# Turning the differential probabilities by VectorE squares and a DRAM round trip in a two-layer attention trunk

## The reference

```python
def diff_attention(q, k, v, lam):            # 4 heads, two 64-dim maps per head
    sc = einsum('bqhcd,bkhcd->bhcqk', qb, kf) * scale      # causal, blocks of 128 queries
    p = softmax(where(causal, sc, -inf))
    attn = p[:, :, 0] - lam * p[:, :, 1]
    return einsum('bhqk,bkhe->bqhe', attn, vf)

def dsa_attention(q, k, v, qi, ki, wi):      # 4 heads of 128; an 8-head indexer picks 64 keys a query
    score = einsum('bqhk,bqh->bqk', relu(einsum('bqhd,bkd->bqhk', qib, kif)), wib)
    _, idx = top_k(where(causal, score, -inf), 64)
    p = softmax(q . k[idx] * scale);  return p @ v[idx]

def hybrid_layer(x, ...):
    h = rms_norm(x);  proj = h @ w_in        # 4680 columns: dq dk dv dg sq sk sv sg iq ik iw
    oa = rms_norm(diff_attention(rope(dq), rope(dk), dv, lam)) * (1 - lambda_init) * silu(dg)
    ob = dsa_attention(rope(sq), rope(sk), sv, rope(iq), rope(layer_norm(ik)), iw) * silu(sg)
    return x + rms_norm(concat(oa, ob) @ w_out)
```

## Time and profile before

| | us |
|---|---|
| median of 3 runs | 302.72 (302.6 to 302.75) |
| the profiled execution | 302.85 |
| its span, first to last instruction | 301.1 |
| PE busy | 292.4 (97%) |
| DVE busy | 234.9 (78%) |
| ACT busy | 163.9 (54%) |
| POOL busy | 67.6 (22%) |
| mean granted TensorE clock | 0.996 of full |

### The profile page before, as it was taken

How to read it: one execution, slowest core, us unless ns; L and a number is a source line. 1 busy time by engine, 2 the same in 40 slices (tenths; PEclk the granted TensorE clock), 3 DMA queues, 4 the chain that set the end, 5 groups by cost and what they waited for, 6 DMA issues and landing times.

```text
span 301.1 us, 4401 instructions
## 1 busy us (share of the span) xinstructions
PE 292.4 (97%) x1568; PEld 246.4 (82%) x1568; DVE 234.9 (78%) x474; ACT 163.9 (54%) x284; POOL 67.6 (22%) x116
## 2 busy tenths in 40 slices
PE   8999999999999999999999999999999999999992
PEld 7799777788787888788888988778878788887892
DVE  4752989899999997955984786878999999787343
ACT  5986963736577473603665855473737747390101
POOL 6558210303030220101060740012303030210101
PEclk9999999999999999999999999999999999999998
DMA  7999959457518569860059799937653675742011
GB/s 242 370 371 386 371 214 354 135 143 227 195 69 210 209 211 303 191 201 23 0 158 369 242 350 250 325 108 204 209 150 131 146 272 152 202 70 72 0 70 70
DMA packets 62229, 60.01 MB, mean 199 GB/s; under 512 B 34560, under 2 KB 39424, under 8 KB 62208
## 3 DMA queue, kind: packets, MB, share of 16 engines
q1 hardware_dynamic: 61920, 59.47, 62.8%
q10 hardware_dynamic: 288, 0.26, 0.3%
...
## 4 chain that ended last, share of the span: by engine, by line
PE 40%; DVE 37%; ACT 8%; DMA 6%; POOL 4%; issue 3%; SPq 1%; POOLq 0%; DVEq 0%; ACTq 0%
DVE w_lo L987 14%; PE bank_a L470 8%; PE bank_a L461 7%; PE bank_a L466 7%; PE bank_s L618 6%; DMA w_raw<-in_w_in 6%; PE bank_a L618 5%; ACT xt_pbuf L831 4%; DVE work L1107 4%; DVE xt_pbuf L1124 3%; DVE top L1106 3%; DVE xt_pbuf L1140 3%; DVE mixn L1150 2%; DVE mixn L1036 2%; PE bank_s L559 1%
## 5 line engine op out<-in xcount | busy, mean ns | idle before, releaser
L987 DVE TENSOR_TENSOR w_lo<-w_raw,w_hi 128x2048 fp32r<-128x2048 f32 (+1 forms) x46 | 98.8, 2154 | 18.5 <-ACT w_hi L763 18.3
L763 ACT ACTIVATE w_hi<-w_raw 128x2048 fp32r<-128x2048 f32 (+1 forms) x46 | 81.9, 1784 | 31.9 <-PE bank_a L470 23.4
L461 PE MATMUL bank_a<-w_hi,h_hi 128*128 128x512 f32 (+1 forms) x272 | 72.5, 388 | 0.0
L470 PE MATMUL bank_a<-w_lo,h_hi 128*128 128x512 f32 (+1 forms) x272 | 70.0, 379 | 0.5 <-DVE w_lo L987 0.5
L466 PE MATMUL bank_a<-w_hi,h_lo 128*128 128x512 f32 (+1 forms) x272 | 69.9, 379 | 0.0
L470 PEld LDWEIGHTS bank_a<-w_lo,h_hi 128*128 128x128 f32 x272 | 49.7, 188 | 10.5 <-DVE w_lo L987 1.0
L466 PEld LDWEIGHTS bank_a<-w_hi,h_lo 128*128 128x128 f32 x272 | 49.8, 188 | 9.8
L461 PEld LDWEIGHTS bank_a<-w_hi,h_hi 128*128 128x128 f32 x272 | 47.9, 188 | 10.4 <-issue 2.7
L831 ACT ACTIVATE xt_pbuf<-xt_pbuf,st 128x128 f32<-128x128 f32 (+1 forms) x48 | 21.3, 444 | 25.1 <-DVE st L1124 25.1
L1417 POOL TENSOR_TENSOR rt<-nat,tab 128x256 f32<-128x256 f32 x10 | 7.4, 741 | 112.5 <-ACT nat L815 112.5
L815 ACT ACTIVATE nat<-bank_a,st 128x512 f32<-128x512 f32 x20 | 13.5, 681 | 19.6 <-PE bank_a L470 19.6
...
## 6 DMA issues: line engine op xcount, KB each, us to landing
...
w_raw<-in_w_in SPq DMA_DIRECT2D x2, 512.0 KB, 6.3
xres<-in_x SPq DMA_DIRECT2D x2, 512.0 KB, 9.5
dqT<-turned SPq DMA_DIRECT2D x2, 512.0 KB, 5.9
```

The lines of the kernel that those rows point to most:

```text
L461: pe.matmul(bank, h_hi[:, HALF * half + kk, tok], whi[:, kk, :], start=half == 0 and kk == 0, stop=False)
L470: mm = pe.matmul(bank, h_hi[:, HALF * half + kk, tok], wlo[:, kk, :], start=False, stop=half == 1 and kk == HALF - 1)
L763: act.activation(unit(w_hi, u), unit(raw, u), ACT.Copy).then_inc(hi_done.sem, 1)
L987: dve.tensor_tensor(unit(w_lo, u), unit(raw, u), unit(w_hi, u).bitcast(F32), ALU.subtract).then_inc(lo_done.sem, 1)
```

## The change

The three differential probability tiles (PD0 for block 0; PD1A and PD1B for the two head pairs of block 1) go the way of the sparse ones: DVE squares (into `mixn`'s first half and the two halves of `nat` slot 1), four DMAs to DRAM, one DMA back to `pT`. PE's `turn_probs` and DVE's three `drain`s fall away. Other work gets new places:

- `turn_squares` of the sparse q writes to `iqT` and not to `mixn`; the copy of the turned sparse keys into the same memory therefore waits for that put.
- On DVE, the sparse keys' drain and `mask_scores(12)` come ahead of parts of `choose` and of `split_lo(18)`, and `split_lo(20)` to `split_lo(22)` come later.
- On ACT, `move(15)` stands ahead of `exps(10)`.
- On SP, the get of the sparse q comes ahead of the load of unit 20, and the three new puts and gets stand between the loads of units 20, 21 and 22.
- On PE, `values(0)` and `values(1)` come later, T_MD1 and T_MS0 stand together ahead of `values(3)`, and `values(3)` comes ahead of `out_part(1, 0, 0)`.

```diff
-T_IK, T_DK, T_PD0, T_PD1A, T_SK, T_PD1B = 4, 5, 7, 8, 9, 11
-T_MD0, T_MD1, T_MS0, T_MS1 = 12, 13, 14, 15
-T_USES = 16
-PS0, PS1 = range(3, 5)
+T_IK, T_DK, T_SK = 4, 5, 7
+T_MD0, T_MS0, T_MD1, T_MS1 = 9, 10, 11, 12
+T_USES = 13
+IQS, DQS, SQS, PD0, PD1A, PD1B, PS0, PS1 = range(8)
+SLOT = {PD0: 0, PD1A: 1, PD1B: 2, PS0: 0}
...
-        prob_buf = {PS0: dkT[:, 0:2, :].rearrange("p f t -> p (f t)"), PS1: dqT[:, :, :, :].rearrange("p b f t -> p (b f t)")}
+        prob_buf = {PD0: mixn[:, 0, :], PD1A: nat[:, 1, 0, :], PD1B: nat[:, 1, 1, :], PS0: dkT[:, 0:2, :].rearrange("p f t -> p (f t)"), PS1: dqT[:, :]}
...
             def get_probs(layer, n):
                 sp.wait_ge(prob_put[n].sem, prob_put[n].at(layer, 16 * SQUARES))
-                sp.wait_ge(o_filled.sem, o_filled.at(layer, 1 if n == PS0 else 2))
-                dst = pT[:, 0, :] if n == PS0 else pT[:, 1:3, :].rearrange("p s n -> p (s n)")
-                sp.dma_start(dst, scratch[n].rearrange("p a t -> p (a t)")).then_inc(prob_landed[n].sem, 16)
+                if n >= PS0:
+                    sp.wait_ge(o_filled.sem, o_filled.at(layer, 1 if n == PS0 else 2))
+                dst = pT[:, 1:3, :].rearrange("p s n -> p (s n)") if n == PS1 else pT[:, SLOT[n], :]
+                sp.dma_start(dst, scratch[n].rearrange("p s t -> p (s t)")).then_inc(prob_landed[n].sem, 16)
...
                     if u == 16:
                         sp.wait_ge(sq_squares.sem, sq_squares.at(layer, 1))
-                        put(2, squares, sq_put.sem)
+                        put(SQS, iqT, sq_put.sem)
+                        sp.wait_ge(sq_put.sem, sq_put.at(layer, 16 * SQUARES))
+                        get(SQS, sqT, sq_landed.sem)
                     if u == 17:
-                        sp.wait_ge(sq_put.sem, sq_put.at(layer, 16 * SQUARES))
-                        get(2, sqT, sq_landed.sem)
+                        put_probs(layer, PD0)
+                        put_probs(layer, PD1A)
+                        get_probs(layer, PD0)
+                    if u == 18:
+                        put_probs(layer, PD1B)
+                        get_probs(layer, PD1A)
+                        get_probs(layer, PD1B)
...
                 for u in range(RING):
                     if u == 0:
                         put_probs(layer, PS0)
+                        get_probs(layer, PS0)
                     if u == 1:
-                        get_probs(layer, PS0)
-                    if u == 2:
                         put_probs(layer, PS1)
                         get_probs(layer, PS1)
...
-                pe.wait_ge(combined.sem, combined.at(layer, 1))
-                turn_probs(T_PD0, 6, 0, HEADS)
                 diff_scores(10, 1, (2, 3))
                 second(15)
-                pe.wait_ge(combined.sem, combined.at(layer, 2))
-                turn_probs(T_PD1A, 8, 1, 2)
                 first(16)
                 second(16)
                 turn_nat(T_SK, 0, 5)
                 first(17)
-                pe.wait_ge(combined.sem, combined.at(layer, 3))
-                turn_probs(T_PD1B, 10, 1, 2)
                 pe.wait_ge(t_drained.sem, t_drained.at(layer, T_SK + 2))
                 pe.wait_ge(sq_landed.sem, sq_landed.at(layer, sq_landed.per_layer))
                 dsa_scores(12, 0, range(HEADS))
-                pe.wait_ge(t_drained.sem, t_drained.at(layer, T_PD0 + 1))
-                values(0, 0, v_diff, [[slot(0, h)] for h in range(HEADS)], place(layer, DV, 0) + 1)
                 second(17)
                 first(18)
+                pe.wait_ge(prob_landed[PD0].sem, prob_landed[PD0].at(layer, 16))
+                values(0, 0, v_diff, [[gathered(pT[:, 0, :], h, slots=HEADS)] for h in range(HEADS)], place(layer, DV, 0) + 1)
                 dsa_scores(13, 1, (0, 1))
                 dsa_scores(14, 1, (2, 3))
-                pe.wait_ge(t_drained.sem, t_drained.at(layer, T_PD1B + 1))
-                values(1, 1, v_diff, [[slot(1 + h // 2, 2 * (h % 2) + t) for t in range(2)] for h in range(HEADS)],
+                second(18)
+                pe.wait_ge(prob_landed[PD1A].sem, prob_landed[PD1A].at(layer, 16))
+                pe.wait_ge(prob_landed[PD1B].sem, prob_landed[PD1B].at(layer, 16))
+                values(1, 1, v_diff, [[gathered(pT[:, 1 + h // 2, :], 2 * (h % 2) + t, slots=HEADS) for t in range(2)] for h in range(HEADS)],
                        place(layer, DV, 1) + 1)
-                second(18)
+                first(19)
                 turn_mix(T_MD0, 0, 0)
-                first(19)
                 second(19)
-                turn_mix(T_MD1, 1, 1)
-                pe.wait_ge(prob_landed[PS0].sem, prob_landed[PS0].at(layer, 16))
-                values(2, 0, v_dsa, [[slot(0, h)] for h in range(HEADS)], place(layer, SV, 0) + 1)
+                pe.wait_ge(proj_moved.sem, proj_moved.at(layer, place(layer, SV, 0) + 1))
                 pe.wait_ge(t_drained.sem, t_drained.at(layer, T_MD0 + 1))
                 out_part(0, 0, 0)
-                turn_mix(T_MS0, 0, 2)
+                pe.wait_ge(prob_landed[PS0].sem, prob_landed[PS0].at(layer, 16))
+                values(2, 0, v_dsa, [[gathered(pT[:, 0, :], h, slots=HEADS)] for h in range(HEADS)], place(layer, SV, 0) + 1)
                 pe.wait_ge(proj_moved.sem, proj_moved.at(layer, GROUPS))
                 out_part(0, 0, 1)
+                turn_mix(T_MS0, 0, 2)
+                turn_mix(T_MD1, 1, 1)
+                pe.wait_ge(prob_landed[PS1].sem, prob_landed[PS1].at(layer, 16))
+                values(3, 1, v_dsa, [[gathered(pT[:, 1:3, :].rearrange("p s n -> p (s n)"), 2 * h + t) for t in range(2)] for h in range(HEADS)],
+                       place(layer, SV, 1) + 1)
                 pe.wait_ge(t_drained.sem, t_drained.at(layer, T_MS0 + 1))
                 out_part(1, 0, 0)
-                pe.wait_ge(prob_landed[PS1].sem, prob_landed[PS1].at(layer, 16))
-                values(3, 1, v_dsa, [[slot(1 + h // 2, 2 * (h % 2) + t) for t in range(2)] for h in range(HEADS)],
-                       place(layer, SV, 1) + 1)
                 out_part(1, 0, 1).then_inc(y_done.sem, 1)
...
                 move(14)
                 split_hi(layer, 18)
+                move(15)
                 exps(10, 1, 2)
                 exps(11, 1, 2)
-                move(15)
                 split_hi(layer, 19)
...
-                    dve.wait_ge(exps_done.sem, exps_done.at(layer, use + 1 - S_DIFF0))
-                    probs = pbuf[:, 0, :] if n == PS0 else pbuf[:, 1:3, :].rearrange("p s n -> p (s n)")
+                    if n >= PS0:
+                        dve.wait_ge(exps_done.sem, exps_done.at(layer, use + 1 - S_DIFF0))
+                    else:
+                        dve.wait_ge(combined.sem, combined.at(layer, n - PD0 + 1))
+                    probs = pbuf[:, 1:3, :].rearrange("p s n -> p (s n)") if n == PS1 else pbuf[:, use % 4, :]
...
                 mask_scores(9, 1, 2, causal[:, :])
+                turn_squares(1, 4, sq_squares.sem)
                 dve.wait_ge(dq_put.sem, dq_put.at(layer, 16 * SQUARES))
-                turn_squares(1, 4, sq_squares.sem)
+                turn_probs(PD0, 6)
                 split_lo(layer, 16)
                 combine(8, 1, 2, 0)
-                drain(T_PD0, pT[:, 0, :])
+                dve.wait_ge(sq_squares.sem, sq_squares.at(layer, 1))
+                turn_probs(PD1A, 8)
                 mask_scores(10, 1, 2, causal[:, :])
                 mask_scores(11, 1, 2, causal[:, :])
                 split_lo(layer, 17)
+                combine(10, 1, 2, 2)
+                turn_probs(PD1B, 10)
+                dve.wait_ge(sq_put.sem, sq_put.at(layer, 16 * SQUARES))
+                drain_pair(T_SK, skT)
                 choose(1, 2)
-                drain(T_PD1A, pT[:, 1, :])
-                combine(10, 1, 2, 2)
+                mask_scores(12, 0, 4, work[0][:, :])
+                split_lo(layer, 18)
                 choose(1, 1)
                 mask_unchosen(1)
-                drain_pair(T_SK, skT)
-                split_lo(layer, 18)
-                drain(T_PD1B, pT[:, 2, :])
-                mask_scores(12, 0, 4, work[0][:, :])
+                turn_probs(PS0, 12)
                 split_lo(layer, 19)
-                turn_probs(PS0, 12)
-                split_lo(layer, 20)
-                gate_diff(0)
-                split_lo(layer, 21)
                 mask_scores(13, 1, 2, work[1][:, :])
                 mask_scores(14, 1, 2, work[1][:, :])
+                gate_diff(0)
+                split_lo(layer, 20)
                 turn_probs(PS1, 14)
                 dve.wait_ge(subln_ready.sem, subln_ready.at(layer, 1))
                 drain_mix(T_MD0, m_hi, m_lo, 0, subln)
                 gate_diff(1)
+                split_lo(layer, 21)
+                gate_dsa(0)
                 split_lo(layer, 22)
+                drain_mix(T_MS0, h_hi, h_lo, 0)
                 drain_mix(T_MD1, m_hi, m_lo, 1, subln)
-                gate_dsa(0)
```

(1 more changed line is left out.)

62 lines of the change are left out of this document (29 added, 33 removed).

## The result

The changed kernel takes **312.4 us** (median of 4 runs, 309.7 to 314.0) against 302.7: a ratio of 1.031, 95% interval 1.027 to 1.035. The forecast was 300.3, its range 298.5 to 303.8.

A forecast was written before the change was run, and what follows sets the result against it. PE was taken as the bound: 302.85 (profiled execution) - 2.8 for turns - 1.4 for holes + 1.4 for a wait at values(3) + 0.4 for split_lo(23) = 300.45, as a median 300.3 us; range 298.5 to 303.8.

The forecast's parts named there:

- What bounds the kernel: Whole kernel: PE is the bound, busy 292.4 of 301.1 us, so work taken from it counts in full.
- PE's removed work, 2.8 + 1.4: On PE: six turns of 0.47 removed save 2.8 us; two holes of 0.70 ahead of T_MS0 go, 1.4.
- Rival (d): DVE bounds the same stretch, so each gain turns into a wait: 302.7 us; chance 0.14 together with Rival (c).
- DVE: DVE's copies become squares at no cost; only split_lo(23) comes late, a 0.3 to 0.4 us wait at out_part(1, 0, 1).
- The rope: Sparse keys' rope on POOL stands until split_lo(17) ends, then ends at 98.9, in time for T_SK at 99.1.
- Rival (c): POOL and DVE hold each other up longer; PE waits 1.0 us a layer at T_SK: 302.3; chance 0.14 with Rival (d).
- if the rope wins: Port contention between DVE and POOL's rope: DVE is late by about 0.8 us, keys' copy keeps 0.5 of cover.
- The walk through SP and the DMA engines: First layer's queue times: PS1 lands at 130.9, PE wants it at 129.6; values(3) waits 1.4 us.
- rival (b): Queue slower than walked; values(3) waits 4.7 us in the first layer, 1.7 in the second: 304.9; chance 0.18.
- The wait taken at its own length: Waits on PE counted at their length alone, 1.4 and 0.4 us, with the granted clock expected to stay at 1.00.
- the sign of a wrong queue walk: In the changed kernel's trace: the wait on pT appears in values(1) or values(2), or in both layers.

The follow-up runs named there:

- the reordered kernel: Changed kernel with only SP's order edited: PD0's puts ahead of unit 20, PS0's ahead of unit 23, PS1's trip ahead of the next layer's first load; 300.1 us.
- the last experiment: Against the reordered kernel, two DVE edits: PD1A's squares behind split_lo(17), and split_lo(23) ahead of the copy of T_MD1; 298.75 us.
- The first experiment: Changed kernel with one edit: values(3) stands behind out_part(1, 0, 0) again, as before the change; 308.5 us.
- the filled waits: Changed kernel with throwaway products on PE: eight ahead of values(3) in the first layer, six ahead of values(1) in the second; 309.3 us.
- the tail alone: Changed kernel with PS0's puts ahead of unit 23's load, PS0's get and PS1's trip ahead of the next layer's first load; PD0's puts unmoved; 302.1 us.

## Why the prediction was wrong, point by point

**What bounds the kernel: right.** PE does, and where nothing it needs is late, most of the work taken off shows (put back into the reordered kernel, the 2.8 us of turns cost 2.0).

**PE's removed work, 2.8 + 1.4: right in size, conditional in kind.** The arrivals in the reordered kernel match to 0.3 us once its earlier start is counted, and without new waits the time is 4.1 below before (4.2 forecast). Rival (d), every gain becomes a wait, is what happens when the turns go alone (303.1), though by its own reason only in part: the new wait is mostly for POOL's rope, not for DVE.

**DVE: right.** The 0.3 to 0.4 us at `out_part(1, 0, 1)` are there: 0.45 in the second layer of the changed kernel, 0.45 in the first of the reordered one (132.16 + 2 x 0.91 = 133.99, started 134.44).

**The rope: off by 0.45 us.** POOL's timeline in the changed kernel:

```profile
96.03 2.49 POOL L1419 TENSOR_TENSOR rt<-nat,tab 128x128 f32<-128x128 f32 x1
```

The third operation met `split_lo(17)` and stood through it (2.49 in place of 0.46), as foreseen, but the fourth then began at 98.60 and needed its own 0.75: it ended at 99.35, not 98.9, and T_SK started at 99.40, 0.3 late. Small, and part of what the last experiment gave back.

**Rival (c): not its wait, but its other half.** `combine(10)` did meet the rope's last operation, and it was DVE that stood. DVE's timeline:

```profile
98.64 0.72 DVE L1137 SCALAR_TENSOR_TENSOR st<-st 128x2 f32<-128x2 f32 x1
```

It ends with the rope's fourth operation (99.36 and 99.35) and took 0.22 where no rope ran (at 92.68); with L1135 before it (0.42 in place of 0.14) `combine(10)` is 0.8 us late. That is the 0.8 of the prediction's "if the rope wins", and the cover held: the keys' copy ended at 102.20 and PE came at 103.08.

**The walk through SP and the DMA engines: this step failed.** It had every trip and their order. The times of the first layer:

| on SP | forecast (worst) | changed kernel | reordered kernel |
|---|---|---|---|
| get PD0 | 102.3 | 105.82 | 101.08 |
| puts of PD1B end | 105.9 | 109.68 | 106.00 |
| unit 22 | 109 to 111 | 114.29 | 110.70 |
| puts of PS0 start | 111.5 to 112.3 | 115.32 | 111.17 |
| get PS0 | 118.8 (121.5) | 125.16 | 118.97 |
| puts of PS1 start | 119.6 (122.6) | 126.02 | 119.36 |
| get PS1 | 127.3 (130.7) | 134.05 | 125.11 |

Up to PS1's puts, the forecast's column is nearly that of the kernel with the *other* order, by coincidence: the walk had the loads in the changed kernel's places and priced them too low. Two terms were too small: the eight puts behind unit 20 took 9.4 us, where I had 5.6 (7.7 to 8.0 in three other executions, below); and PS0's trip, with two loads ahead of it, took 9.84 from the first put to the get (115.32 to 125.16), where I had 7.3, from the 6.8 of the earlier trace rows with one load ahead. And the bounds opened by only 3.4 us over all five trips, while the slips add up, since each late trip also delays the loads and with them the next: 6.75 us at the last get, twice the worst that I allowed. The sentence that rival (b) "needs every rate at its slow end" was wrong: loads ahead of the trips were enough, as the same transfers in another order show.

**The wait taken at its own length: too small.** 1.7 us per long wait, for the granted clock, were in no term. I had expected the clock to stay at 1.00.

**Rival (b)** had the sign, the place and the mechanism, at 304.9: 4.7 and 1.7 us of waits against the 10.8 measured at `values`, and no 3.4 us for the clock. It had a chance of 0.18. What the text named as the sign of a wrong queue walk is what came: a wait in `values(1)` and `values(2)`, and in both layers.

**What stays open.** The changed kernel's runs lie 4.3 us apart and the reordered one's 1.0. The traces show one place that varies. The first experiment, the filled waits and the tail alone have the changed kernel's order on SP up to the get of PD0; there the eight puts behind unit 20 took 7.7 to 8.0 us in the first layer and 7.7 to 8.4 in the second, against 9.4 and 9.6 in the profiled changed kernel. Its 3.5 us of wait at `values(1)` in the second layer go with that: the first experiment had 0.6 there, the tail alone 0.9. Why the puts take longer in one execution than in another is open. So is why the small pieces cost some 3.7 us while the landing of the first put stays at 5.6.
